# Joining the gating values and the second input projection into one program part, in a two-block kernel on one Trainium2 core

## The chip, the core and the metric

The kernel runs on one core of a Trainium2 chip. A core has five engines with their own instruction queues: TensorE (PE in the profile, its weight loads PEld), VectorE (DVE), ScalarE (ACT), GpSimd (POOL) and SyncE (SP, which here only issues DMAs). They meet at semaphores. The metric is the device time of one execution in microseconds (us); lower is better. Three runs of the kernel before took 3345.0, 3327.26 and 3340.97 us, with a median of 3340.97. The profiled execution took 3344.58 us, of which the trace spans 3342.8.

## The reference

Two residual blocks work on x, 2048 tokens of width 1024. The first is banded attention beside a multi-scale pooling, each gated; the second is a long convolution (Hyena) beside a spatial gating unit (SGU). Cut to what matters:

```python
def first_block(x, ...):
    h = rmsnorm(x, pre_norm_g)
    q, k, v, g_a, u_p, g_p = split(h @ w_in)
    a = banded_attention(q, k, v, rel_bias, attn_sink) * silu(g_a)
    p = multiscale_pool(u_p, pool_w, pool_scale) * silu(g_p)
    mixed = concat([a, p]) @ w_out                # "first output projection"
    return x + rmsnorm(mixed, post_norm_g)

def second_block(x, ...):
    proj = rms_norm(x, pre_norm_w) @ w_in         # 1024 -> 7168
    hy_in, hy_gate, sg_u, sg_v, sg_gate = split(proj)
    x0, x1, v = split(short_conv_centred(hy_in, conv_w, conv_b))
    k = hyena_filter(L, ...)      # three sine layers of width 64, exact to fp32
    y_a = x0 * long_conv_bidir(v * x1, k, hyena_skip) * silu(hy_gate)
    vn = normalise sg_v over the 128 values of each head
    y_b = sg_u * (sgu_w @ vn + sgu_b) * silu(sg_gate)
    return x + rms_norm(concat([y_a, y_b]) @ w_out, post_norm_w)
```

All is fp32. To multiply in TensorE's one-pass format (fp32r) without losing digits, an operand is split into a high part (ScalarE copies it to the format) and a low part (VectorE subtracts the copy from the value), and a product becomes three matmuls: high·high, low·high, high·low.

## The kernel before

The program is a row of parts. Each part is one block in which all engines run their own list of instructions; between two blocks stands a barrier. The parts are `first_block`, then two blocks in `second_inputs` (the gating values; the second input projection), `long_convolution` and `output`.

**End of `first_block`: the first output projection.** The 2048 tokens are 16 groups of 128 (`NT`). For group i TensorE runs `mix`, 48 matmuls of 128x512 (L849 to L851) into two of four banks of PSUM, then the 8 transposes (L729) of the *previous* group. After `mix` of a group ScalarE squares and sums (L520), GpSimd makes the reciprocal root from it (L400, L403), VectorE scales (L706) and adds the residual (L709, `x1_done`). Then ScalarE squares again (L522), GpSimd makes the second root, ScalarE scales (L526, `hs_done`), TensorE transposes, and VectorE takes the transposed tokens out of PSUM (L541). The features of group i+2 are split on the way: ScalarE copies (`features_high`, L492, L493; the second half comes from a scratch in DRAM by the DMA L362) and VectorE subtracts (`features_low`, L676, L677). VectorE also does 6 or 7 operations per group of `first_layer` (a sine for the filter net, L944 to L960), which have nothing to do with the tokens but must be done by the end of the part. The order of all of it is that of the code. Before the first `mix`, features and weights of the output projection are split (`weights_high` L485, `weights_low` L672), while the last of the 32 attention steps still runs: ScalarE takes the turned probabilities out of PSUM (L505), TensorE multiplies them (L832), VectorE gates the result (`gate`, L658).

**`second_inputs`, first block: gating values.** 32 steps (2 halves of 512 columns, 16 token groups) of 24 matmuls each (L1384 to L1386) go into one of six banks of PSUM in turn. VectorE takes mean and variance (L1353, L1358), GpSimd the root (L1282, L1284), VectorE the offset (L1367, `nb_done`), ScalarE normalises four heads out of PSUM (L1313, `vn_done`), SyncE stores. In the steps VectorE also does `SV_OPS[s]` operations of the filter's second layer (`filter_op`: L109 to L132, 631 in all); SyncE loads their rows (L66).

**`second_inputs`, second block: projection.** 49 tiles in a list: for each of 8 heads `gate`, `u`, `mix`, then for each of 8 groups `x0`, `hgate`, `x1`, `v`, with `third` (the filter's third layer) before the last group's. A tile of weights is 96 matmuls (L1665 to L1667) into four banks; tiles take banks 0 to 3 and 4 to 7 in turn. The weights (`WR`, two slots) are split two tiles ahead: ScalarE L1508, VectorE L1562. VectorE works on each tile (L1572, L1575, L1599 to L1615) and then does `OPS_BY[kind]` filter operations (13, for `mix` 6); whatever is left of the 631 it does at `x0` of group 6, and there `second_angle` follows (L1580, L1677 to L1687, L1582).

The SBUF place of the split value weights (`WVH`, `WVL`) is handed to the split weights of the projection (`WH2`, `WL2`) and to its buffers (`MB`) when the first of the two blocks ends.

Of the kernel before, what the change touches and what calls it, by code (L numbers as in the profile page):

```python
# [13 lines left out]
P = 128  # L14
# [120 lines left out]
def first_block(nc, A, M, WOH, WOL, FH, FL, PS, x1_d, h1_d, h2_d):  # L135


    with ExitStack() as ctx:
# [288 lines left out]
        def _(s):  # L427
# [69 lines left out]
            for st, (n, g) in enumerate(STEPS):  # L497
# [17 lines left out]
            for i in range(NT):  # L515
# [13 lines left out]
        def _(v):  # L529
# [169 lines left out]
            for i in range(NT):  # L699
# [397 lines left out]
def second_inputs(nc, A, PS, behind, CC, HP, kept, h1_d, h2_d, vn_d, bi_d, u_d, gx_d, yb_d):  # L1097

    with ExitStack() as outer:
# [84 lines left out]
        with ExitStack() as ctx:  # L1184
            def stage_sem(name):
                return ctx.enter_context(nc.semaphore(name))

# [3 lines left out]
            const_in = stage_sem("c2_in")  # L1191
            bias_in = stage_sem("bias2_in")
            hh_in = [stage_sem("hh_in%d" % i) for i in range(4)]
            high_done = stage_sem("high_done")
            low_done = stage_sem("low_done")
            sv_done = stage_sem("sv_done")
            quarter_done = stage_sem("quarter_done")
            stats_done = stage_sem("stats_done")
            var_done = stage_sem("var_done")
            rstd_done = stage_sem("rstd2_done")  # L1200
            nb_done = stage_sem("nb_done")
            vn_done = stage_sem("vn_done")
            vn_stored = [stage_sem("vn_stored%d" % i) for i in range(2)]
            bias_mm = stage_sem("bias2_mm")
            bias_done = stage_sem("bias2_done")
            bias_stored = stage_sem("bias2_stored")

            STEPS = 2 * NT
            block = ctx.enter_context(nc.Block())

            @block.sync
            def _(sp):
# [54 lines left out]
                for b in range(2):  # L1267
                    sp.wait_ge(vn_stored[b], 16 * NT)
                sp.wait_ge(bias_stored, 16)

            @block.gpsimd
            def _(g):
# [13 lines left out]
            @block.scalar  # L1286
            def _(s_):
# [27 lines left out]

            @block.vector
            def _(v):
# [21 lines left out]
                for s in range(STEPS):  # L1339
                    if s == 6:  # L1340
                        v.wait_ge(bias_mm, 2)
                        v.wait_ge(bias_in, 48)
                        for x in range(2):
                            v.tensor_tensor(BIA[:, 4 * x:4 * x + 4], PS[:, 6 + x, :].rearrange("p (a b) -> p a b", b=P),
# [3 lines left out]
                    if s in (NT - 1, NT):  # L1348
                        values_low(4 + 2 * (s - NT + 1))
                        values_low(5 + 2 * (s - NT + 1))  # L1350
                    v.wait_ge(sv_done, s + 1)
                    for a in range(4):
                        v.bn_stats(ST[:, a], PS[:, s % 6, P * a:P * a + P]).then_inc(stats_done, 1)  # L1353
# [16 lines left out]
            @block.tensor  # L1370
            def _(t):
                def quarter(s, q):
# [8 lines left out]
                    dst = PS[:, s % 6, :]  # L1381
# [1199 lines left out]
```

## Time and profile before

| | |
|---|---|
| Median of 3 runs | 3340.97 us (3327.26 to 3345.0) |
| Profiled execution | 3344.58 us, span 3342.8 us |
| TensorE busy | 3086.8 us, 92% of the span |
| VectorE busy | 2504.9 us, 75% |
| ScalarE busy | 804.9 us, 24% |
| GpSimd busy | 299.0 us, 9% |
| First output projection | from about 793.7 to 1027.6 us |
| Gating values | TensorE from 1045.7 to about 1239.1 us |
| Projection | TensorE from 1257.7 to about 2377 us |

Busy shares are means over parts with different limits. In a row of the trace, the number in square brackets is how long the engine stood idle before the instruction, and the name behind the arrow is the engine, tile and line that ended this wait. PEclk (granted clock) is 1.00 where TensorE runs at 2.4 GHz and 0.50 where it runs at 1.2 GHz; in between it is a mixture of the two.

### The profile page before, as it was taken

What the parts mean: (1) busy time and instruction counts of PE and PEld (TensorE: products, weight loads), DVE (VectorE), ACT (ScalarE), POOL (GpSimd) and SP (SyncE); (2) the same over time, 40 slices, a digit from 0 to 9 for tenths busy, and PEclk for the clock granted to TensorE, in tenths of its full rate; (3) what the DMA queues carried; (4) which work ended last, traced back from release to release, by engine and by line L of the source; (5) the groups of instructions that cost most, each with busy time, mean ns of one, the idle gap of its engine ahead of it and who ended that gap; (6) DMA issues with size and microseconds to landing.
All of it is one profiled execution on the core that took longest, in us unless ns stands there. A gap on an engine that the chain in (4) does not pass through costs nothing. (4 is left out here: it accounts for less than half of the span.)

```text
span 3342.8 us, 33360 instructions
## 1 busy us (share of the span) xinstructions
PE 3086.8 (92%) x13138; PEld 2238.6 (67%) x13138; DVE 2504.9 (75%) x2672; ACT 804.9 (24%) x1394; POOL 299.0 (9%) x420
## 2 busy tenths in 40 slices
PE   6999999889885989999999999999898999979999
PEld 4444444656774767787888888787566666777887
DVE  6979999597995796999999999975456667552221
ACT  2000000585333321000011111112353735431110
POOL 3211220000112350000000000000000000000000
PEclk9999999999997999999999999999999999979999
DMA  6565551201437454665545454521211120334321
GB/s 202 145 178 149 141 149 44 108 1 54 133 129 225 136 151 120 162 179 156 162 139 145 136 141 134 143 76 34 112 54 51 54 101 13 138 116 142 100 88 53
DMA packets 206060, 392.21 MB, mean 117 GB/s; under 512 B 20224, under 2 KB 132032, under 8 KB 198032
## 3 DMA queue, kind: packets, MB, share of 16 engines
q1 hardware_dynamic: 186000, 319.27, 31.2%
q0 software_dynamic: 18752, 62.42, 7.3%
q10 hardware_dynamic: 1152, 8.39, 0.7%
q8 instruction: 104, 1.70, 0.2%
q14 instruction: 52, 0.43, 0.0%
HBM read 312.41 MB, written 81.81 MB: 118 GB/s over the span
## 5 line engine op out<-in xcount | busy, mean ns | idle before, releaser
L1665 PE MATMUL PS<-HH,WH 128*128 128x512 f32 x1536 | 605.4, 394 | 40.2 <-DVE WL L1562 23.0
L1667 PE MATMUL PS<-HH,WL 128*128 128x512 f32 x1536 | 604.9, 394 | 0.0
L1666 PE MATMUL PS<-HL,WH 128*128 128x512 f32 x1536 | 604.2, 393 | 0.0
L782 PE MATMUL PS<-M 128*128 128x512 f32 x1152 | 502.3, 598 | 16.2 <-DVE M L605 13.6
L782 PEld LDWEIGHTS PS<-M 128*128 128x128 f32 x1152 | 220.4, 192 | 297.4 <-issue 279.8
L1665 PEld LDWEIGHTS PS<-HH,WH 128*128 128x128 f32 x1536 | 290.2, 189 | 110.3 <-DVE WL L1562 19.0
L1666 PEld LDWEIGHTS PS<-HL,WH 128*128 128x128 f32 x1536 | 290.2, 189 | 64.1
L1667 PEld LDWEIGHTS PS<-HH,WL 128*128 128x128 f32 x1536 | 290.3, 189 | 62.9
L109 DVE SCALAR_TENSOR_TENSOR HP<-MF,HP 128x1024 f32<-128x1024 f32 x252 | 323.4, 1283 | 8.0
L2394 PE MATMUL PS<-WH,YH 128*128 128x512 f32 x512 | 200.9, 392 | 14.7 <-DVE WL L2365 9.5
L109 DVE SCALAR_TENSOR_TENSOR M<-M 128x1024 f32<-128x1024 f32 x160 | 205.6, 1285 | 7.2 <-DMA M<-c_feat 1.5
L2395 PE MATMUL PS<-WH,YL 128*128 128x512 f32 x512 | 200.5, 392 | 0.0
L2396 PE MATMUL PS<-WL,YH 128*128 128x512 f32 x512 | 200.3, 391 | 0.0
L2354 DVE TENSOR_TENSOR YL<-KX,YH 128x2048 fp32r<-128x2048 f32 x14 | 32.1, 2292 | 209.3 <-ACT YH L2323 209.3
L1547 ACT ACTIVATE MB<-PS,MF 128x2048 f32<-128x2048 f32 x24 | 49.5, 2064 | 473.8 <-PE PS L1667 435.4
L2045 DVE TENSOR_TENSOR M<-PS,M 128x1024 f32<-128x1024 f32 x64 | 78.4, 1225 | 108.8 <-ACT M L1935 107.9
L2163 PE MATMUL PS<-M 128*128 128x256 f32 x512 | 131.4, 398 | 7.1 <-issue 4.2
L66 POOL DMA_DIRECT2D M<-c_feat x194 | 99.2, 516 | 383.5 <-DVE M L109 361.9
L1384 PE MATMUL PS<-WVH,HH 128*128 128x512 f32 x256 | 103.2, 403 | 28.2 <-DVE HL L1332 23.3
L2394 PEld LDWEIGHTS PS<-WH,YH 128*128 128x128 f32 x512 | 97.0, 189 | 35.3 <-DVE WL L2365 9.7
L2163 PEld LDWEIGHTS PS<-M 128*128 128x128 f32 x512 | 92.2, 188 | 41.7 <-issue 25.1
L2311 POOL MEMSET NEGH<- 128x1 f32 x1 | 0.1, 98 | 1337.3 <-POOLq L1692 1337.3
(220 smaller groups left out, 5110.7 us busy)
## 6 DMA issues: line engine op xcount, KB each, us to landing
MF<-h_scratch SPq DMA_DIRECT2D x380, 256.0 KB, 4.3
M<-c_feat POOLq DMA_DIRECT2D x194, 256.0 KB, 4.3
MF<-w_in SPq DMA_DIRECT2D x56, 512.0 KB, 4.7
M<-u_scratch SPq DMA_DIRECT2D x16, 1024.0 KB, 4.8
M<-w_in SPq DMA_DIRECT2D x18, 512.0 KB, 4.8
M<-x SPq DMA_DIRECT2D x16, 512.0 KB, 4.4
x_scratch<-M SPq DMA_DIRECT2D x16, 512.0 KB, 5.3
h_scratch<-M SPq DMA_DIRECT2D x16, 512.0 KB, 5.8
```

The source lines that it names most:

```text
L66: eng.dma_start(dst[HID * half:HID * half + HID], row).then_inc(loaded, 16)
L109: return v.scalar_tensor_tensor(out=out, in0=a, scalar=s_, in1=b, op0=op0, op1=op1)
L782: ins = t.matmul(PS[:, banks + c, :], wt[:, k], HT[:, k, TC * c:TC * c + TC], start=(k == 0), stop=(k == KD - 1))
L1384: t.matmul(dst, hh, wh, start=(k == 0), stop=False)
L1665: t.matmul(dst, wh, hh, start=(k == 0), stop=False)
L1666: t.matmul(dst, wh, hl, start=False, stop=False)
L1667: ins = t.matmul(dst, wl, hh, start=False, stop=(k == KD - 1))
L2045: v.tensor_tensor(PM, PS[:, bank:bank + 2, :], KS[:, n % 2], ALU.mult).then_inc(pm_done, 1)
L2163: return t.matmul(PS[:, bank, at:at + CH], STRIP[:, 2 * p + x, HID * strip:HID * strip + P], src[:, p, x], start=True, stop=True)
L2394: t.matmul(dst, yh, wh, start=(k == W_ORDER[0]), stop=False)
L2395: t.matmul(dst, yl, wh, start=False, stop=False)
L2396: return t.matmul(dst, yh, wl, start=False, stop=(k == W_ORDER[-1]))
```

## The change

It has three parts.

1. In the first output projection, ScalarE splits the features of group i+2 right behind L520 instead of behind L522, and VectorE does 3 of its 6 or 7 sine operations ahead of `features_low` and the rest behind it. Before the first `mix`, only group 0 and weight part 0 are split ahead of the last attention step; part 1 and group 1 come behind it on both engines.
2. Gating values and projection become one block. The values use banks 2 to 7 instead of 0 to 5 (`2 + s % 6`), the bias banks 0 and 1. In the last value step ScalarE and VectorE split the projection's first two weight tiles as soon as TensorE has finished the quarter of `WVH`/`WVL` whose place they take. TensorE's first tile waits for banks 2 and 3 by `vn_done`. GpSimd and SyncE wait for the last stores of the values before they load into the same places.
3. `SV_OPS` falls from 72 to 52 filter operations in the value steps.

```diff
@@ first_block, scalar
                 if st == len(STEPS) - 2:
...
-                    for i in range(2):
-                        features_high(i)
-                        weights_high(i)
+                    features_high(0)
+                    weights_high(0)
+            weights_high(1)
+            features_high(1)
...
                 s.activation(HS[:, i % 2], ps, ACT.Square, accum_out=SSQ[:, i:i + 1]).then_inc(mssq_done, 1)
+                if i + 2 < NT:
+                    features_high(i + 2)
                 s.wait_ge(x1_done, i + 1)
                 s.activation(HS[:, i % 2], X1[:, i % 2], ACT.Square, accum_out=SSQ2[:, i:i + 1]).then_inc(x1ssq_done, 1)
-                if i + 2 < NT:
-                    features_high(i + 2)
@@ first_block, vector
             gate(len(STEPS) - 2)
-            for i in range(2):
-                features_low(i)
-                weights_low(i)
+            features_low(0)
+            weights_low(0)
             gate(len(STEPS) - 1)
+            weights_low(1)
+            features_low(1)
...
                     features_out(i - 1)
+                first_layer_work(3)
                 if i + 2 < NT:
                     features_low(i + 2)
-                first_layer_work(7 if i < 7 else 6)
+                first_layer_work(4 if i < 7 else 3)
@@ second_inputs, values; scalar and vector
+                    if s == STEPS - 1:
+                        ahead_of_last()
...
-                        s_.activation(CN[s % 2][:, P * a:P * a + P], PS[:, s % 6, P * a:P * a + P], ACT.Identity,
+                        s_.activation(CN[s % 2][:, P * a:P * a + P], PS[:, 2 + s % 6, P * a:P * a + P], ACT.Identity,
@@ values, tensor
-                    if s == NT - 1:
+                    if s in (NT - 1, STEPS - 1):
                         ins.then_inc(quarter_done, 1)
@@ projection, sync
+                values_sync(sp)
...
                 raw_next(0)
                 raw_next(1)
+                for b in range(2):
+                    sp.wait_ge(vn_stored[b], 16 * NT)
@@ projection, gpsimd
+                values_gpsimd(g)
+                for b in range(2):
+                    g.wait_ge(vn_stored[b], 16 * NT)
+                g.wait_ge(sv_done, STEPS)
@@ projection, scalar
-                weights_high(0)
-                weights_high(1)
+                def first_high():
+                    for w in range(2):
+                        s.wait_ge(quarter_done, 5 + w)
+                        weights_high(w)
+
+                values_scalar(s, first_high)
@@ projection, vector
-                weights_low(0)
-                weights_low(1)
+                def first_low():
+                    for w in range(2):
+                        v.wait_ge(quarter_done, 7 + w)
+                        weights_low(w)
+
+                values_vector(v, first_low)
@@ projection, tensor
+                            if j == 0:
+                                t.wait_ge(bias_done, 2)
+                                if c >= 2:
+                                    t.wait_ge(vn_done, 4 * (STEPS - 3 + c))
...
-SV_OPS = [0] * 8 + [3] * 24
+SV_OPS = [0] * 8 + [3] * 8 + [2] * 12 + [1] * 4
```

Three places in the engines' orders follow. The line numbers of the kernel after are up to 16 higher: L520 is L521 there, L522 is L525, L526 is L527, L706 is L708, L709 is L711, L953 is L956, L1313 is L1307, L1508 is L1510, L1562 is L1568, L1353 is L1348. Rows name an instruction and its output and inputs; M is the first block's SBUF buffer, FH and FL are the high and low parts of features, WH and WL those of projection weights, MF and HP hold filter data.

VectorE, first output projection, one token group, before:

```order
L706 SCALAR_TENSOR_TENSOR M<-PS,M 128x1024
L709 TENSOR_TENSOR M<-M 128x1024
L541 TENSOR_TENSOR M<-PS,M 128x1024
L676 TENSOR_TENSOR FL<-M,FH 128x512
L677 TENSOR_TENSOR FL<-FL,FH 128x512
L953 TENSOR_TENSOR M<-M 128x1024 x3
L957 TENSOR_SCALAR M<-M 128x1024
```

And after:

```order
L708 SCALAR_TENSOR_TENSOR M<-PS,M 128x1024
L711 TENSOR_TENSOR M<-M 128x1024
L542 TENSOR_TENSOR M<-PS,M 128x1024
L956 TENSOR_TENSOR M<-M 128x1024 x3
L677 TENSOR_TENSOR FL<-M,FH 128x512
L678 TENSOR_TENSOR FL<-FL,FH 128x512
L960 TENSOR_SCALAR M<-M 128x1024
```

Three sine operations now stand between L541 and the two subtractions of the features.

VectorE, the last two value steps and the start of the projection, before:

```order
L1353 BN_STATS MF<-PS 128x6 x4
L1358 BN_AGGR MF<-MF 128x2 x4
L130 TENSOR_TENSOR MF<-MF,HP 128x1024
L132 TENSOR_TENSOR MF<-HP,MF 128x1024
L109 SCALAR_TENSOR_TENSOR HP<-MF 128x1024
L1367 SCALAR_TENSOR_TENSOR MF<-MF 128x4
L1184 UNCONDITIONAL_BRANCH
L1553 UNCONDITIONAL_BRANCH
L1562 TENSOR_TENSOR WL<-MF,WH 128x1024 x3
```

And after:

```order
L132 TENSOR_TENSOR MF<-HP,MF 128x1024
L1362 SCALAR_TENSOR_TENSOR MF<-MF 128x4
L1568 TENSOR_TENSOR WL<-MF,WH 128x1024 x2
L1348 BN_STATS MF<-PS 128x6 x4
L1353 BN_AGGR MF<-MF 128x2 x4
L109 SCALAR_TENSOR_TENSOR HP<-MF 128x1024
L1362 SCALAR_TENSOR_TENSOR MF<-MF 128x4
L1568 TENSOR_TENSOR WL<-MF,WH 128x1024
```

The branches into the next block are gone, the first two weight tiles stand ahead of the last step's statistics, and one filter operation is left in the step instead of three.

VectorE, projection, tile `x0` of group 6, before:

```order
L1572 SCALAR_TENSOR_TENSOR MB<-PS,MF,MB 128x2047
L1575 SCALAR_TENSOR_TENSOR MB<-PS,MF,MB 128x2047
L1562 TENSOR_TENSOR WL<-MF,WH 128x1024
L1580 TENSOR_SCALAR MF<-MF 128x1024
L1677 TENSOR_SCALAR HP<-MF 128x1024
```

And after:

```order
L1578 SCALAR_TENSOR_TENSOR MB<-PS,MF,MB 128x2047
L1581 SCALAR_TENSOR_TENSOR MB<-PS,MF,MB 128x2047
L1568 TENSOR_TENSOR WL<-MF,WH 128x1024
L132 TENSOR_TENSOR MF<-HP,MF 128x1024
L109 SCALAR_TENSOR_TENSOR HP<-MF 128x1024
L116 TENSOR_TENSOR HP<-HP,MF 128x1024
L118 TENSOR_TENSOR MF<-HP 128x1024
L120 TENSOR_TENSOR MF<-MF 128x1024
L109 SCALAR_TENSOR_TENSOR HP<-MF,HP 128x1024 x4
L130 TENSOR_TENSOR MF<-MF,HP 128x1024
L132 TENSOR_TENSOR MF<-HP,MF 128x1024
L1586 TENSOR_SCALAR MF<-MF 128x1024
```

Eleven filter operations now stand between the weights and `second_angle`; nine more stand at the tile ahead of it (`v` of group 5: 13 instead of 4).

## Rows read from the trace of the kernel before

**Rows 1.** Windows: start:end, length, busy of PE PEld DVE ACT POOL, PEclk, DMA share, GB/s

```profile
1239.10:1257.70 18.60, 0.03 (x1) 0.00 (x0) 11.91 (x28) 6.83 (x15) 8.16 (x7) 0.62 0.51 142
2123.45:2213.86 90.41, 88.40 (x385) 71.96 (x385) 88.38 (x65) 11.86 (x9) 0.00 (x0) 1.00 0.44 122
```

**Rows 2.** Timeline, VectorE, one token group of the first output projection

```profile
880.36 1.28 DVE L706 SCALAR_TENSOR_TENSOR M<-PS,M 128x1024 f32<-128x1024 f32 x1
...
885.16 0.69 DVE L676 TENSOR_TENSOR FL<-M,FH 128x512 fp32r<-128x512 f32 x1 [1.12 <-ACT FH L493]
...
886.37 8.77 DVE L953 TENSOR_TENSOR M<-M 128x1024 f32<-128x1024 f32 x7
895.18 1.28 DVE L706 SCALAR_TENSOR_TENSOR M<-PS,M 128x1024 f32<-128x1024 f32 x1
```

**Rows 3.** Groups of instructions, VectorE, 810 to 1010 us: busy, mean ns, idle before

```profile
L676 DVE TENSOR_TENSOR FL<-M,FH 128x512 fp32r<-128x512 f32 x14 | 9.7, 693 | 16.8 <-ACT FH L493 16.8
```

**Rows 4.** Timeline, ScalarE's scaling in group 5 and in group 14

```profile
885.03 1.15 ACT L526 ACTIVATE M<-M 128x1024 f32<-128x1024 f32 x1
1010.41 1.15 ACT L526 ACTIVATE M<-M 128x1024 f32<-128x1024 f32 x1 [2.79 <-POOL M L403]
```

**Rows 5.** Timeline, GpSimd's root in group 5 and in group 14

```profile
884.45 0.55 POOL L403 TENSOR_TENSOR M<-M 128x1 f32<-128x1 f32 x1
1008.84 1.53 POOL L403 TENSOR_TENSOR M<-M 128x1 f32<-128x1 f32 x1
```

**Rows 6.** Timeline, VectorE, starts of groups 14 and 15

```profile
1003.89 1.28 DVE L706 SCALAR_TENSOR_TENSOR M<-PS,M 128x1024 f32<-128x1024 f32 x1
1015.50 1.28 DVE L706 SCALAR_TENSOR_TENSOR M<-PS,M 128x1024 f32<-128x1024 f32 x1 [0.50 <-POOL M L403]
```

**Rows 7.** DMA issues: KB each, median us to landing, of the features' second half

```profile
FL<-pt_scratch SPq DMA_DIRECT2D x16, 256.0 KB, 5.9
```

**Rows 8.** Timeline, ScalarE and TensorE, last attention step

```profile
787.81 0.62 ACT L492 ACTIVATE FH<-M 128x512 fp32r<-128x512 f32 x1
789.79 0.64 ACT L505 ACTIVATE M<-PS 128x256 f32<-128x256 f32 x2
790.22 1.12 PE L811 MATMUL PS<-M 128*128 128x128 f32 x4 [2.63 <-ACT M L505]
```

**Rows 9.** Timeline, VectorE, first value step: statistics to offset

```profile
1069.52 0.89 DVE L1353 BATCH_NORM_STATS2 MF<-PS 128x6 f32<-128x128 f32 x4 [11.02 <-PE PS L1386]
1073.13 0.17 DVE L1367 SCALAR_TENSOR_TENSOR MF<-MF 128x4 f32<-128x4 f32 x1 [1.19 <-POOL MF L1284]
```

**Rows 10.** Timeline, ScalarE and TensorE, from the values to the projection

```profile
1250.11 1.50 ACT L1313 ACTIVATE CN<-PS,MF 128x128 f32<-128x128 f32 x4 [3.60 <-DVE MF L1367]
1255.36 2.00 ACT L1508 ACTIVATE WH<-MF 128x1024 fp32r<-128x1024 f32 x2 [3.75 <-PEq L1184]
1257.73 0.80 PE L1665 MATMUL PS<-HH,WH 128*128 128x512 f32 x1 [18.60 <-DVE WL L1562]
1281.39 1.88 ACT L1526 ACTIVATE MB<-PS 128x2048 f32<-128x2048 f32 x1 [22.73 <-PE PS L1667]
```

**Rows 11.** Timeline, VectorE, projection, groups 5 and 6

```profile
2122.08 1.22 DVE L1562 TENSOR_TENSOR WL<-MF,WH 128x1024 fp32r<-128x1024 f32 x1
2140.08 2.35 DVE L1572 SCALAR_TENSOR_TENSOR MB<-PS,MF,MB 128x2047 f32<-128x2047 f32 x1
2212.49 1.22 DVE L1562 TENSOR_TENSOR WL<-MF,WH 128x1024 fp32r<-128x1024 f32 x1
2218.78 2.35 DVE L1572 SCALAR_TENSOR_TENSOR MB<-PS,MF,MB 128x2047 f32<-128x2047 f32 x1
2238.04 2.29 DVE L1615 TENSOR_TENSOR MB<-MB 128x2048 f32<-128x2048 f32 x1 [2.60 <-ACT MB L1534]
```

**Rows 12.** Timeline, ScalarE, behind tiles hgate and x1 of group 6

```profile
2236.12 1.88 ACT L1534 ACTIVATE MB<-PS 128x2048 f32<-128x2048 f32 x1 [20.45 <-PE PS L1667]
2258.10 2.06 ACT L1547 ACTIVATE MB<-PS,MF 128x2048 f32<-128x2048 f32 x1 [19.15 <-PE PS L1667]
```

More of the change, by code:

```diff
@@ L1190, in second_inputs, with values_sync @@
             CN = [CC[:, 0:TC], sbuf(ctx, "CN", [TC], F32)[:, :]]
[L1191 to L1206, printed above, removed]
+            const_in = sem("c2_in")
+            bias_in = sem("bias2_in")
+            hh_in = [sem("hh_in%d" % i) for i in range(4)]
+            high_done = sem("high_done")
+            low_done = sem("low_done")
+            sv_done = sem("sv_done")
+            quarter_done = sem("quarter_done")
+            stats_done = sem("stats_done")
+            var_done = sem("var_done")
+            rstd_done = sem("rstd2_done")
+            nb_done = sem("nb_done")
+            vn_done = sem("vn_done")
+            vn_stored = [sem("vn_stored%d" % i) for i in range(2)]
+            bias_mm = sem("bias2_mm")
+            bias_done = sem("bias2_done")
+            bias_stored = sem("bias2_stored")
             STEPS = 2 * NT
-            block = ctx.enter_context(nc.Block())
-            @block.sync
-            def _(sp):
+            def values_sync(sp):
                 def values_load(c):
@@ L1266, in _, with values_gpsimd @@
                         weight_load(sp, 1)
[L1267 to L1272, printed above, removed]
+            def values_gpsimd(g):
                 g.sem_clear(behind)
@@ L1284, in _, with values_scalar @@
                     g.tensor_tensor(RSTD[:, s % 2], RSTD[:, s % 2], NEGH, ALU.pow).then_inc(rstd_done, 1)
-            @block.scalar
-            def _(s_):
+            def values_scalar(s_, ahead_of_last):
                 def values_high(c):
@@ L1312, in _, with values_vector @@
                     for a in range(4):
-                        s_.activation(CN[s % 2][:, P * a:P * a + P], PS[:, s % 6, P * a:P * a + P], ACT.Identity,
+                        s_.activation(CN[s % 2][:, P * a:P * a + P], PS[:, 2 + s % 6, P * a:P * a + P], ACT.Identity,
                                       bias=NB[:, s % 2, a:a + 1], scale=RSTD[:, s % 2, a:a + 1]).then_inc(vn_done, 1)
-            @block.vector
-            def _(v):
+            def values_vector(v, ahead_of_last):
                 def values_low(c):
@@ L1343, in _ @@
                         for x in range(2):
-                            v.tensor_tensor(BIA[:, 4 * x:4 * x + 4], PS[:, 6 + x, :].rearrange("p (a b) -> p a b", b=P),
+                            v.tensor_tensor(BIA[:, 4 * x:4 * x + 4], PS[:, x, :].rearrange("p (a b) -> p a b", b=P),
                                             SGBA[:, 4 * x:4 * x + 4], ALU.add).then_inc(bias_done, 1)
@@ L1350, in _ @@
                         values_low(5 + 2 * (s - NT + 1))
+                    if s == STEPS - 1:
+                        ahead_of_last()
                     v.wait_ge(sv_done, s + 1)
                     for a in range(4):
-                        v.bn_stats(ST[:, a], PS[:, s % 6, P * a:P * a + P]).then_inc(stats_done, 1)
+                        v.bn_stats(ST[:, a], PS[:, 2 + s % 6, P * a:P * a + P]).then_inc(stats_done, 1)
                     v.wait_ge(stats_done, 4 * s + 4)
@@ L1368, in _, with values_tensor @@
                                            op0=ALU.mult, op1=ALU.mult).then_inc(nb_done, 1)
-            @block.tensor
-            def _(t):
+            def values_tensor(t):
                 def quarter(s, q):
@@ L1380, in quarter @@
                         t.wait_ge(wl_done, 4 * half + q + 1)
-                    dst = PS[:, s % 6, :]
+                    dst = PS[:, 2 + s % 6, :]
                     for k in (2 * q, 2 * q + 1):
@@ L1393, in values @@
                         ins = quarter(s, q)
-                    if s == NT - 1:
-                        t.wait_ge(quarter_done, 4)
+                    if s in (NT - 1, STEPS - 1):
+                        t.wait_ge(quarter_done, 4 * (s // NT + 1))
                         t.sem_inc(sv_done, 1)
@@ L1412, in _ @@
                     for a in range(4):
-                        ins = t.matmul(PS[:, 6 + x, P * a:P * a + P], SNBA[:, 4 * x + a], SGTA[:, 4 * x + a], start=True, stop=True)
+                        ins = t.matmul(PS[:, x, P * a:P * a + P], SNBA[:, 4 * x + a], SGTA[:, 4 * x + a], start=True, stop=True)
                     ins.then_inc(bias_mm, 1)
@@ L1628, in _ @@
             def _(t):
+                values_tensor(t)
                 def banks_free(j):
```

2 lines of the change are left out of this document (removed).

## The prediction

> **What bounds the kernel now.** I read the windows by stage first, then VectorE's timeline in the first output projection, then the three engines around the barrier between values and projection, and last VectorE's timeline near the end of the filter work, because that is where moved work must come out again. TensorE is busy 92% of the span, so what is left to win are its waits; each part has its own.
>
> In the first output projection VectorE sets the pace. One token group (group 5) runs from 880.36 to 895.18, 14.82 us, and in it VectorE stands idle once, 1.12 us, for ScalarE's copy of the features; the seven sine operations after it are back to back, and the next group starts at once [rows 2]. Over the stretch these waits are 16.8 us in 14 pieces, the first of them longer than the others [rows 3].
>
> Between values and projection TensorE stands 18.60 us. ScalarE normalises the last step at 1250.11 and begins the first weight tile of the next block at 1255.36; TensorE starts at 1257.73 [rows 10]. The window over the gap shows a granted clock of 0.62, so TensorE fell from 2.4 to 1.2 GHz in it [rows 1], and the first tile took 1281.39 - 1257.73 = 23.66 us [rows 10] where a regular one takes 2258.10 - 2236.12 = 21.98 [rows 12].
>
> In the projection both engines are full: in the 90.41 us of one group of four tiles TensorE is busy 88.40 and VectorE 88.38 [rows 1]. There is no room for more VectorE work until the filter is done. That comes at `x0` of group 6; from L1615 on VectorE waits, the first time 2.60 us [rows 11].
>
> **The change part by part.** Sums are made against the profiled execution, 3344.58 us.
>
> *Start of the output projection.* ScalarE took the last step's probabilities out at 789.79; the second batch of splitting ahead of it began at 787.81 [rows 8]. With the batch behind it, they come out 1.98 us sooner, and TensorE, which waited 2.63 us for them [rows 8], goes on sooner by as much. What could be late next is the weights: weight part 1 and one features split now stand behind VectorE's gate. A part serves 6 matmuls, 21.98 / 16 = 1.37 us at full clock, and VectorE makes one in about 1.2 us, so it keeps ahead except at the first parts, where TensorE's clock has just come out of a wait. Bounds 0 and 2.0, a little more if the clock no longer falls in the wait; I take -2.0, since the chain is plain.
>
> *ScalarE's copies ahead of L522, three sine operations ahead of `features_low`.* This takes the 16.8 us [rows 3] off VectorE: the copies are done while it works on the group before. All its instructions stay. What is late next:
> - GpSimd's second root. In group 5 it took 0.55 us in its second instruction, and ScalarE scaled at 885.03, 4.67 us after the group's start; in group 14, which has no features to wait for, VectorE was working meanwhile, the same instruction took 1.53, and ScalarE scaled 1010.41 - 1003.89 = 6.52 us after the start [rows 2, 4 to 6]. VectorE will now always be working there, so I take 6.52. The next group can start at the earliest 1015.50 - 1010.41 = 5.09 us later (the next square, its root), 11.61 after its forerunner, as group 15 did, with 0.50 of idle time [rows 6]. VectorE itself needs 14.82 - 1.12 = 13.70 us with seven sine operations and 1.25 less, 12.45, with six [rows 2]. It stays the slowest by 0.8.
> - TensorE. `features_low` ends at 3.68 (885.16 - 1.12 - 880.36) + 3 x 1.25 + 1.21 = 8.6 us after the group's start, the transposes about when 6.52 + 1.15 + 1 = 8.7. Its own work is 48 matmuls (half a tile, 11.0) and the transposes (about 1): 12.0, under 12.45.
> I take 16.8 less 0.3, for group 1's and group 15's roots, which now show: -16.5. Bounds: -16.8, and 0 if the chain of roots takes over (below).
>
> The Trainium skill has a rule that speaks against this step: by the GPSIMD Engine Reference, Key points, GpSimd shares its SBUF interfaces with VectorE and contends with VectorE instructions that have two SBUF inputs. The trace agrees (0.55 against 1.53 us). Were the rule without effect the chain would be 9.8 instead of 11.6, and the sum the same, since 12.45 is above both.
>
> *Joining the blocks.* TensorE ends the values at 1257.73 - 18.60 = 1239.13 [rows 10]; the last step of 24 matmuls (5.5 us) begins at 1233.6. With one filter operation per step VectorE no longer lags, so step 30 goes as in the first step: 1073.13 - 1069.52 = 3.61 us from the statistics to the offset, with one operation of that size between [rows 9], then 0.2 and 1.50 for ScalarE's normalising [rows 10]: 1238.9. Only then does ScalarE come to the new first weight tile (its queue is in order; the tile's place has been free since 1235). From ScalarE's start to TensorE's it was 1257.73 - 1255.36 = 2.37 us [rows 10]: 1241.3. TensorE stands 2.2 us instead of 18.6: -16.4. I take it that the clock then holds, and the tile 1.7 us shorter: -18.1 together. What else waits there: banks 2 and 3 need steps 30 and 31 normalised, 1238.9 and about 1248, while TensorE wants them 11 and 16.5 us after 1241.3. SyncE's loads for tiles 2 and 3 stand behind the last store (about 1248) and are wanted after tile 0, at 1263; GpSimd's loads for `mix` stand behind the stores' landing and are wanted at 1285. Bounds: -14 (the root as slow as with a busy VectorE, and the clock falls) and -20.3 (no gap at all).
>
> *Twenty filter operations moved.* In the values they cost nothing: TensorE sets the pace there. In the projection the full price is 20 x 1.30 = 26 us of VectorE. (1.30: from weights to next taps it is 18.00 us with 13 operations, 6.29 with 4 [rows 11], so 11.7 for nine.) Up to `v` of group 5 every tile has the same number as before. There it is 13 instead of 4: the taps of `x0` 6 go from 2218.78 to 2230.5. The weights of `x1` are then ready at 2230.5 + 2 x 2.35 + 1.2 = 2236.4 or so, TensorE wants them at 2236.1: 0.5 late. From these taps to L1615 it was 2238.04 - 2.60 - 2218.78 = 16.66; with 11 more operations (14.3) L1615 is at 2261.5 and the weights of `v` are ready at 2261.5 + 2.2 + 1.2 = 2264.9. TensorE ends `x1` at 2258.6, so it stands 6.3 us; before it went on at 2258.1 [rows 12]. That is +6.8, and +1.7 for the clock after such a wait: +8.5. From there VectorE has slack of over 10 us per tile. Bounds: +5 (half of it, if the clock holds and operations pair better) and +27.7 (all 26 and the clock).
>
> Sum: -2.0 - 16.5 - 18.1 + 8.5 = **-28.1 us**, 3316.5 for an execution like the profiled one. The median of the runs shown is 3.6 us below that one, so I predict 3340.97 - 28.1 = **3312.9 us**.
>
> **Rivals.**
> 1. *The moved operations come at full price.* For it: VectorE is at 88.38 of 90.41 us. Against: the idle time after L1615 takes up what isn't due earlier. -2.0 - 16.5 - 18.1 + 27.7 = -8.9: 3332 us.
> 2. *The roots' chain takes VectorE's place in the first output projection.* For it: margin of only 0.8 us, and GpSimd's time changes with what VectorE does [rows 5]. Against: group 14 shows the chain with VectorE busy, 11.61. At 13.6 us a group nothing is won: -11.6, 3329 us.
> 3. *The seam opens less than it seems*, because another wait (the table load, a load behind the stores, step 31's normalising) holds the first tiles. About 12 us of the 18 lost: -16, 3325 us.
> 4. *Slower: ScalarE waits for the features' DMA.* The copies now stand ahead of L522, and their second half needs a DMA that is issued when `mix` of the group before ends, 8.7 + 11.0 - 12.45 = 7.3 us into the group. With a landing of 5.9 us [rows 7] and 0.6 for the copy ScalarE is free at 13.8, 1.3 into the next group, and L522 is wanted at 2.5. So a landing of 7.1 us is where it begins to cost, every microsecond above it 14 times. At 11 us it is 14 x 3.9 = 55: +27, 3368 us. Against: 5.9 was measured with three other transfers in flight; the DMA now goes out alone.
>
> **How the numbers follow.** The forecast 0.72 (its own range 3304 to 3321), rivals 1, 2 and 3 0.08 each, rival 4 0.03, 0.01 for the rest. The range of 8 in 10 takes in part of the rivals and the runs' own scatter: 3301 to 3328. A difference under 0.5% (16.7 us) can't be told from none. Faster by more than that (below 3324.3) are the forecast, nearly all of it, and a good third of rivals 2 and 3 in milder form: 0.79. Within: 0.18. Slower: 0.03.
>
> **What would show it.** VectorE: no idle time ahead of the features' subtraction, groups of 13.7 and 12.4 us, ScalarE's scaling 6.5 us into the group. Seam: TensorE idle 2 to 3 us, first tile near 22 us. Group 6: TensorE's wait for the weights of `v` about 6 us, TensorE at 1.2 GHz for the first matmuls behind it. Wrong would be: VectorE waiting for GpSimd at L706 in most groups, ScalarE waiting for the DMA ahead of L493's copy, waits of TensorE for L1562 in the gate, u and mix tiles longer than before, or a seam over 6 us.

## The result and the profile after

The kernel after takes **3314.22 us** (median of 8 runs, 3298.07 to 3317.83), the one before 3335.47 (8 runs, 3326.84 to 3345.0). The ratio is 0.9926, 95% interval 0.9903 to 0.995. The profiled execution took 3317.83 us (span 3316.0) against 3344.58 (span 3342.8): -26.75, where the sum had said -28.1. Of the sixteen runs of before beside experiments 1 to 4 and 7, one took 12136.62 us; it is left out, and the median given there is that of the other fifteen.

| place | before | after | moved by | forecast |
|---|---|---|---|---|
| near the end of attention (gate of the fifth step from the last) | 778.76 | 780.40 | +1.64 | none |
| first group of the output projection begins | 808.36 | 807.24 | -2.76 | -2.0 |
| its sixteenth group begins | 1015.50 | 996.23 | -18.15 | -16.5 |
| TensorE begins the values | 1045.67 | 1026.18 | -0.22 | none |
| TensorE ends the values | 1239.13 | 1222.02 | +2.38 | none |
| TensorE begins the projection | 1257.73 | 1224.15 | -16.47 | -16.4 |
| end of its tile 0 | 1281.39 | 1246.43 | -1.38 | -1.7 |
| end of `v`, group 6 | 2280.08 | 2254.05 | +8.93 | +8.5 |
| long convolution begins | 2387.32 | 2361.01 | -0.28 | none |
| end of the span | 3342.8 | 3316.0 | -0.5 | none |

The fourth column is what the stretch up to that place gave or took by itself; its sum is -26.8.

**A group of the output projection.** VectorE's timeline of one after (start in us, duration in us, engine and line, operation, out<-in, partitions x elements, count, and in brackets the idle time before it with what ended it):

```profile
872.03 1.28 DVE L708 SCALAR_TENSOR_TENSOR M<-PS,M 128x1024 f32<-128x1024 f32 x1
873.35 1.23 DVE L711 TENSOR_TENSOR M<-M 128x1024 f32<-128x1024 f32 x1
874.49 1.22 DVE L542 TENSOR_TENSOR M<-PS,M 128x1024 f32<-128x1024 f32 x1
875.63 3.74 DVE L956 TENSOR_TENSOR M<-M 128x1024 f32<-128x1024 f32 x3
879.40 0.69 DVE L677 TENSOR_TENSOR FL<-M,FH 128x512 fp32r<-128x512 f32 x1
880.01 0.68 DVE L678 TENSOR_TENSOR FL<-FL,FH 128x512 fp32r<-128x512 f32 x1
880.61 4.99 DVE L956 TENSOR_TENSOR M<-M 128x1024 f32<-128x1024 f32 x4
885.64 1.28 DVE L708 SCALAR_TENSOR_TENSOR M<-PS,M 128x1024 f32<-128x1024 f32 x1
```

L677 has no bracket: the 1.12 us of before [rows 2] are gone, and the group takes 885.64 - 872.03 = 13.61 us instead of 14.82. ScalarE's scaling and GpSimd's root in it, and VectorE where the last group begins:

```profile
878.55 1.15 ACT L527 ACTIVATE M<-M 128x1024 f32<-128x1024 f32 x1 [2.78 <-POOL M L403]
```

```profile
876.98 1.53 POOL L403 TENSOR_TENSOR M<-M 128x1 f32<-128x1 f32 x1
```

```profile
996.23 1.28 DVE L708 SCALAR_TENSOR_TENSOR M<-PS,M 128x1024 f32<-128x1024 f32 x1 [0.50 <-POOL M L403]
```

The scaling comes 878.55 - 872.03 = 6.52 us into the group, where it came after 4.67 [rows 2, 4], and the root takes 1.53 us, where it took 0.55 [rows 5]. In this group before, the root ran while VectorE stood idle for the copy; now VectorE is in the middle of its sine operations. The later scaling costs nothing, since VectorE needs 12.35 us and more. Only the sixteenth group waits, by the same 0.50 as before [rows 6].

ScalarE now waits ahead of its copies, which it did not do before:

```profile
882.30 0.63 ACT L492 ACTIVATE FH<-M 128x512 fp32r<-128x512 f32 x1 [1.60 <-issue]
```

"issue" means that the profile shows no releaser. The wait is for the DMA of the features' second half: issued at 878.39, it landed at 882.23, 0.07 us ahead of this row, and in 13 of the 14 groups the copy starts 0.07 to 0.08 us behind the landing. The waits are 26.0 us in sum, none above 2.5. They cost nothing, because both copies end at 883.5, before ScalarE's second square of the next group can start, at 888.2.

**The seam.** ScalarE, VectorE and TensorE, in that order, around the end of the values:

```profile
1220.32 1.51 ACT L1307 ACTIVATE CC<-PS,MF 128x128 f32<-128x128 f32 x4 [2.84 <-DVE MF L1362]
1221.70 2.01 ACT L1510 ACTIVATE WH<-MF 128x1024 fp32r<-128x1024 f32 x2
...
1246.43 1.88 ACT L1532 ACTIVATE MB<-PS 128x2048 f32<-128x2048 f32 x1 [14.57 <-PE PS L1683]
```

```profile
1222.87 2.36 DVE L1568 TENSOR_TENSOR WL<-MF,WH 128x1024 fp32r<-128x1024 f32 x2 [2.59 <-ACT WH L1510]
```

```profile
1224.15 0.50 PE L1681 MATMUL PS<-HH,WH 128*128 128x512 f32 x1 [2.13 <-DVE WL L1568]
```

The chain is the same as in [rows 10], from ScalarE's copy to TensorE 1224.15 - 1221.70 = 2.45 us, but it begins before TensorE is done with the values, not 16 us behind. The first matmul takes 0.50 us, where it took 0.80 [rows 10], and the window (columns as in [rows 1]) shows the full grant, 2.4 GHz, where [rows 1] had 0.62. That the clock held is this execution's; experiments 5 and 7 have the same wait and lost it (below).

```profile
1218.00:1224.00 6.00, 4.03 (x18) 2.89 (x16) 2.17 (x3) 3.40 (x6) 1.94 (x2) 1.00 0.28 96
```

**Group 6 of the projection**, where the moved filter work comes out: VectorE, then TensorE, then the clock.

```profile
2195.41 2.35 DVE L1578 SCALAR_TENSOR_TENSOR MB<-PS,MF,MB 128x2047 f32<-128x2047 f32 x1
2197.79 2.35 DVE L1581 SCALAR_TENSOR_TENSOR MB<-PS,MF,MB 128x2047 f32<-128x2047 f32 x1
2200.18 1.23 DVE L1568 TENSOR_TENSOR WL<-MF,WH 128x1024 fp32r<-128x1024 f32 x1
2201.32 1.22 DVE L132 TENSOR_TENSOR MF<-HP,MF 128x1024 f32<-128x1024 f32 x1
...
2226.15 2.28 DVE L1625 TENSOR_TENSOR MB<-MB 128x2048 f32<-128x2048 f32 x1
2228.35 1.22 DVE L1568 TENSOR_TENSOR WL<-MF,WH 128x1024 fp32r<-128x1024 f32 x1
```

```profile
2201.55 0.47 PE L1681 MATMUL PS<-HH,WH 128*128 128x512 f32 x1 [0.48 <-DVE WL L1568]
2229.72 0.77 PE L1681 MATMUL PS<-HH,WH 128*128 128x512 f32 x1 [5.94 <-DVE WL L1568]
```

```profile
2231.00:2244.00 13.00, 13.00 (x51) 10.46 (x51) 5.54 (x3) 1.48 (x2) 0.00 (x0) 0.88 0.36 103
```

Between the weights of `x1` (2200.18) and those of `v` (2228.35) VectorE has 24.8 us of filter work without a gap. TensorE waits 0.48 us for the first and 5.94 for the second, and begins behind the second at 0.77 us a matmul, 1.2 GHz. In a group before that nothing has changed: the same 90.4 us as in [rows 1] give 88.40 and 88.37.

```profile
2103.00:2193.40 90.40, 88.40 (x386) 71.96 (x385) 88.37 (x65) 11.86 (x8) 0.00 (x0) 1.00 0.49 134
```

### The profile page after: what moved, and what is told of

Read it like the earlier page. It is cut to its first block and busy times, and to the rows that moved or that the text cites. A ratio compares the mean times of both kernels' runs of the same rounds, so it can differ in the third digit from the quotient of the medians.

```text
span 3316.0 us, 33371 instructions
## 1 busy us (share of the span) xinstructions
PE 3086.2 (93%) x13138; PEld 2234.5 (67%) x13138; DVE 2503.2 (75%) x2672; ACT 808.8 (24%) x1394; POOL 325.4 (10%) x420
## 5 line engine op out<-in xcount | busy, mean ns | idle before, releaser
L1378 PE MATMUL PS<-WVH,HH 128*128 128x512 f32 x256 | 104.3, 407 | 27.2 <-DVE HL L1325 22.3
```

Of the source, the lines that this page charges most:

```text
L1378: t.matmul(dst, hh, wh, start=(k == 0), stop=False)
```

## The experiments

Every set of runs has its own runs of the kernel before beside it. They lie in two clusters, some 15 us apart, as do those of after and of several kernels below; experiments 8 to 11 are about these. A single execution is compared by stages, not by its total.

**1 and 2. The first block alone.** Starts and groups of the output projection as after; the two old program parts and the old row of filter operations.

```
 weights_high(1)
 features_high(1)
...
-SV_OPS = [0] * 8 + [3] * 8 + [2] * 12 + [1] * 4
+SV_OPS = [0] * 8 + [3] * 24
```

> Only the first part of the change: the new order of splitting and sine operations in the first output projection; two blocks, old SV_OPS. My theory: its gain stands by itself, since the next part begins behind a barrier. From the trace after, the groups run 18.2 us faster and the start about 2.8, so the projection of values begins 20 to 21 us sooner in relation to the attention, the gap of 18.6 us between the blocks stays, and the total is 17 to 21 us under before. Rival (the roots' chain takes over, or the gain is given back at the barrier by late transfers): under 12 us.

Measured: 3314.29 us (median of 10), before 3331.74, ratio 0.9948 (0.9929 to 0.9967). The sixteen groups begin within 189.01 us, as after (188.99), and the seam stays: TensorE waits 18.36 us at 1222.57. But from there to the wait of group 6 it took 1037.85 us, before 1029.23, though no wait is longer than in before and the full clock is shown; the tiles of group 6 took 22.40 us. So the same kernel ran again.

> The same kernel as the first experiment (the first block's new order alone), looked at again for the second projection's tiles, which took 22.4 instead of 22.0 us there with no wait and a full clock shown. Theory (a property of that execution or chip, not of the kernel): the tiles take 22.0 us, first L1668 to the end of the projection 1029 to 1031 us, and the execution is 3305 to 3309 us, or 3321 to 3325 with the late store. Rival (it belongs to this kernel's code): again 22.4 us and 1037 to 1038.

Measured: 3308.6 us, and

```profile
1221.61 0.80 PE L1668 MATMUL PS<-HH,WH 128*128 128x512 f32 x1 [18.55 <-DVE WL L1565]
...
2250.84 0.79 PE L1668 MATMUL PS<-HH,WH 128*128 128x512 f32 x1 [5.02 <-DVE MB L1578]
```

2250.84 - 1221.61 = 1029.23, as before. So the lost 8.6 us belonged to that execution, not to the code: 28 of its tiles in a row ran at 0.233 us a matmul (start to start) instead of 0.229. The second execution has three such tiles, the other traces none to three; what makes a tile 22.40 us in one stretch and 21.98 in another stays open. The first block's part is worth what its stages say, some 21 us (2.76 + 18.15): 3308.6 is 21 us below 3329.75, the middle of the lower cluster of before beside it. The seam and the moved operations give the rest.

**3. The join with the old row of filter operations.**

```
-SV_OPS = [0] * 8 + [3] * 8 + [2] * 12 + [1] * 4
+SV_OPS = [0] * 8 + [3] * 24
```

> The changed kernel with SV_OPS as before (72 filter operations in the value steps, none moved). My theory: VectorE is then some 10 us behind TensorE at the end of the values, and since the split of the first weight tile stands behind its steps, TensorE waits 9 to 10 us at the seam instead of 2.1, with the clock fallen (first tile 23.7 instead of 22.3 us); in return the wait of 5.9 us at v of group 6 is gone. Sum within 3 us of the changed kernel. Rival (moved operations cost their full 26 us): 15 us or more faster than the changed kernel.

Measured: 3298.57 us (median of 7), before 3331.74, ratio 0.9919 (0.9886 to 0.9951).

```profile
1213.20 0.80 PE L1681 MATMUL PS<-HH,WH 128*128 128x512 f32 x1 [9.70 <-DVE WL L1568]
```

With the old row TensorE still waits 9.70 of the 18.6 us: three operations a step keep VectorE late with the statistics, so ScalarE begins to normalise step 30 only at 1209.37, 5.9 us behind the end of the values (1203.51), and its copies are in order behind that. In group 6 the wait for `v` is gone. So the new row trades 7.6 us and a fallen clock at the seam for 5.9 us and a fallen clock in group 6. The two kernels differ by less than these runs can tell.

**4 and 5. Which half of the group's new order does it.** One kernel has ScalarE's two copies behind the second square again, the other VectorE's two rests ahead of all sine operations.

```
 s.activation(HS, ps, Square)
-features_high(i + 2)
 ...
 s.activation(HS, X1, Square)
+features_high(i + 2)
```

```
-first_layer_work(3)
 features_low(i + 2)
-first_layer_work(4 if i < 7 else 3)
+first_layer_work(7 if i < 7 else 6)
```

> The changed kernel with ScalarE's copies of the features behind the second square again, as before; VectorE keeps three sine operations ahead of the subtraction. My theory: VectorE asks for the copies about 7.4 us into a group and they are done at 4.8, so the 16.8 us of waits stay gone, and GpSimd's second root runs beside a busy VectorE all the same: time and group periods as in the changed kernel (13.6 and 12.35 us). Rival (the copies' early place is what counts): waits of about 1 us a group come back.

> The new block of the output projection's groups with ScalarE's two copies ahead of the two squares, but VectorE's three rests (L677) ahead of all seven of its sine operations, as before the change. Theory (the wait was for ScalarE's copies, and either half alone removes it): no row of L677 waits, the groups keep the periods of after (12.5 and 13.6 us), first to sixteenth L708 within 1 us of 189.0, and the span lies within 4 us of that with VectorE's half alone (3296.4) or, with the late store, 16 to 19 us above. Rival (the halves are not equal: with the rests early VectorE still waits for the second copy, some 1 to 3 us in a group, because both copies need the first square's end): L677 waits 8 to 20 us in sum and the span is longer by that.

Measured: 3298.23 and 3301.9 us, one run each. Groups of instructions on VectorE over the output projection (busy, mean ns, idle before), first of the one with VectorE's half, then of the one with ScalarE's:

```profile
L677 DVE TENSOR_TENSOR FL<-M,FH 128x512 fp32r<-128x512 f32 x14 | 9.7, 692 | 0.5
```

```profile
L677 DVE TENSOR_TENSOR FL<-M,FH 128x512 fp32r<-128x512 f32 x14 | 9.5, 682 | 0.0
```

In [rows 3] it was 16.8 us of idle time. First to sixteenth group take 189.02 and 188.97 us: either half alone brings the whole gain, and the other adds nothing to it. One edit closes the gap between copy and use, whichever side moves; the rival that the halves are unequal fell.

**6. The seam's last 2 us.** ScalarE makes the first weight tiles' copies one value step earlier.

```
-if s == STEPS - 1:
+if s == STEPS - 2:
     ahead_of_last()
```

> After, with one condition changed: ScalarE makes the high halves of the first two weight tiles of the joined section at the last step but one of the values instead of the last. Theory (the 2.1 us at the seam are the tail of a chain ScalarE scaling, ScalarE copies, VectorE rests, and nothing else): TensorE's wait ahead of the first L1681 is 0 to 0.5 us, the clock stays 1.00, and first L1681 to the end of tile 0 is 22.0 to 22.3 us; worth 1.6 to 2.1 us. Rival (the weights' DMA or VectorE's rests are the later condition): the wait stays over 1.5 us. Everything else as in after.

Measured, one run of 3296.42 us:

```profile
1201.65 0.47 PE L1681 MATMUL PS<-HH,WH 128*128 128x512 f32 x1 [0.30 <-PE PS L1380]
```

The wait goes from 2.13 to 0.30, and what ends it is TensorE's own last matmul of the values. Nothing but ScalarE's place in its queue held it. The three other kernels with this edit (experiments 9 to 11) show the same 0.30.

**7. The wait in group 6.** The filter's second pair of sines, 10.7 us of VectorE (2215.48 to 2226.15), is made one tile later, in the gate of group 6.

```
 if (kind, n) == ("x0", 6):
     filter_work(v, OPS_OF(HID))
-    second_angle()
+elif (kind, n) == ("hgate", 6):
+    second_angle()
```

> The changed kernel with second_angle moved from x0 of group 6 to hgate of group 6, behind its gating and its weights. My theory: the 5.9 us that TensorE waits for the weights of v of group 6 is the angle's 10.7 us standing ahead of them, not the moved filter operations as such; with the angle behind, the weights are ready before TensorE ends x1, the wait is 0 to 0.5 us and the clock doesn't fall: 7 to 9 us faster than the changed kernel. Rival (VectorE's total work up to the third tile sets the time): the wait comes back at the next tile and under 3 us are won.

Measured: 3294.89 us (median of 4), before 3331.74, ratio 0.9884 (0.9846 to 0.9922). ScalarE behind `v` of group 6, here and in the kernel of experiment 4, which began the projection within 0.2 us of it:

```profile
2231.21 2.06 ACT L1553 ACTIVATE MB<-PS,MF 128x2048 f32<-128x2048 f32 x1 [15.13 <-PE PS L1684]
```

```profile
2238.62 2.06 ACT L1553 ACTIVATE MB<-PS,MF 128x2048 f32<-128x2048 f32 x1 [21.62 <-PE PS L1683]
```

The wait of 5.9 us and its slow matmuls are gone, -7.4, and the long convolution begins 7.1 us sooner. Of the moved operations' cost this is nearly all: from the first matmul of the projection to the long convolution it is 1130.13 us here and 1129.59 in before, both with a fallen clock in the first tile. The moved operations cost because, with the second pair of sines, they stand ahead of the weights of `v`, not because VectorE lacks the time.

This kernel and that of experiment 4 also show that the wait at the seam can go either way with the clock. After the same 2.13 us the first matmul took 0.50 us there and 0.80 here:

```profile
1208.02 0.80 PE L1682 MATMUL PS<-HH,WH 128*128 128x512 f32 x1 [2.12 <-DVE WL L1568]
```

Tile 0 took 22.3 us there, in after and in experiment 8, and 23.8 here and in experiment 5.

**8 and 9. Two clusters.** The last two sets have 22 runs of before: 10 at 3326.08 to 3332.39, 12 at 3341.65 to 3349.09. After has 6 at 3314 to 3318 and 2 at 3298. Both profiled executions belong to the upper one. VectorE in the first projection, before and after:

```profile
189.86 4.69 DVE L583 TENSOR_TENSOR M<-M 128x2079 f32<-128x2079 f32 x2 [17.41 <-DMA pt_scratch<-M]
```

```profile
192.39 4.68 DVE L584 TENSOR_TENSOR M<-M 128x2079 f32<-128x2079 f32 x2 [19.41 <-DMA pt_scratch<-M]
```

It waits for the 1-MB store of pooled features, which landed 18.2 and 20.3 us after its issue at 171.58 and 171.97. In those of experiments 1 to 7 it landed in 5.0 to 5.1 us (issue at 170.60 to 171.02) and VectorE waited 2.7 or less. At the same moment SyncE issues a 4-MB copy of the output weights inside DRAM (18 us). The idea was that the copy alone makes the store late.

```
-if j == 6:
+if j == 7:
     sp.dma_start(wo_d, A["w_out"][0])
```

> After with one edit: the 4-MB copy of the output weights (L341) is issued one projection tile later. Theory (the two clusters of times, 3298 and 3314 us, come from the 1-MB store of pooled features landing in 5 or in 18 to 20 us, the latter when the copy starts at the same moment): all executions lie in 3294 to 3300, L584 never waits for the store, and the store lands in 4.5 to 6 us. Rival (something else makes the store late): both clusters remain. Rival B (the copy disturbs another load at its new place): one cluster, but above 3300.

> After with three edits: the second sine pair of group 6 made in the tile of its gate (as in the run with the second angle at hgate), the first weight tiles split one step early, and the 4-MB copy of the output weights issued one projection tile later, away from the store of the pooled features. Theory: each takes away its own wait, 7.2, about 2 and, in the executions that have the late store, 15 to 17 us; so all executions lie in one cluster, at 3288 to 3295 us, and the ratio to before is 0.986 to 0.989. Rival A (the late store has another cause than the copy beside it): times stay two-valued, 3290 and 3306. Rival B (the copy at its new place delays the loads of the projection's weights or the second store by as much): one cluster at 3300 to 3310.

Measured: 3307.7 us (4 runs, 3302.07 to 3314.28), and with the edits of experiments 6 and 7 added 3295.25 (6 runs, 3291.09 to 3304.53), before 3341.65, ratios 0.9905 (0.9874 to 0.9937) and 0.9868 (0.984 to 0.9897). Neither theory held. The first is as its rival B said, everything above 3300; the second is two-valued, four runs at 3291 to 3296 and two at 3304, near what its rival A said. VectorE of the first, then of the second:

```profile
217.63 1.28 DVE L109 SCALAR_TENSOR_TENSOR M<-M 128x1024 f32<-128x1024 f32 x1 [1.37 <-DMA M<-c_feat]
219.98 2.60 DVE L109 SCALAR_TENSOR_TENSOR M<-M 128x1024 f32<-128x1024 f32 x2 [1.07 <-DMA M<-c_feat]
```

```profile
181.30 4.68 DVE L584 TENSOR_TENSOR M<-M 128x2079 f32<-128x2079 f32 x2 [8.52 <-DMA pt_scratch<-M]
...
216.73 3.92 DVE L109 SCALAR_TENSOR_TENSOR M<-M 128x1024 f32<-128x1024 f32 x3 [7.16 <-DMA M<-c_feat]
```

At its new place the copy holds up GpSimd's loads of the filter's features instead: those issued within 3 us behind it took 14 to 18 us, undisturbed ones some 4. And the second execution still had the late case, smaller: 9.4 us for a store with no copy beside it. What all four late ones share (before, after, experiment 9, experiment 10) is their start. The first 192 matmuls of the first projection (that of the first block), of after and of experiment 6:

```profile
56.13 84.36 PE L785 MATMUL PS<-M 128*128 128x512 f32 x192 [1.32 <-DVE M L542]
```

```profile
56.71 82.67 PE L785 MATMUL PS<-M 128*128 128x512 f32 x192 [1.32 <-DVE M L542]
```

84.36 us in each of the four, 82.67 in each of the other nine; the window 56 to 83.4 shows a granted clock of 0.94 and of 1.00. The store waits for TensorE, GpSimd's loads for VectorE. With the slow start the store is issued behind the first of the loads (load 170.70, store 171.97 in after), otherwise ahead of them (store 171.02, load 171.16 in experiment 6). That this order makes it late is argued from the times, not tried; why the clock falls at the start in some executions stays open.

**10 and 11. Copy after the last tile, and the same kernel with the copy where it was.** Both have the edits of experiments 6 and 7.

```
-if j == 6:
+if j == n1 - 1:
     sp.dma_start(wo_d, A["w_out"][0])
```

> After with the second sine pair of group 6 made in the tile of its gate, the first weight tiles split a step early, and the 4-MB copy of the output weights issued at the last tile of the first projection (some 490 us, where the DMA share falls to 0.4 and then 0). What the runs so far showed of the late case: TensorE starts the first projection with a fallen clock (first 192 matmuls in 84.4 instead of 82.7 us), so the store of pooled features is issued behind GpSimd's loads, and VectorE, which has no slack there, waits 8.5 us for it without the copy beside it and 19.4 us with it; a copy moved by one tile makes VectorE wait at the second store. Theory: with the copy far away the early case is as in the run with the split a step early or a little better, 3287 to 3293 us, and the late one 8 to 11 us above it (3296 to 3303) instead of 16. Rival: the late store doesn't depend on the copy; the clusters stay 15 to 17 us apart.

> As the run with the copy after the last tile, but with the copy where the kernel after has it. Theory: two clusters, 3288 to 3294 and 3304 to 3310 us. Rival: the seam's edit gives back 2 us and no more, the second angle's is hidden: 3292 to 3298 for the early cluster.

Measured: with the copy late 3293.75 us (6 runs, 3290.26 to 3296.68), with the copy in its old place 3291.41 (4 runs: 3284.54, 3291.03, 3291.79, 3307.73), before 3344.62; ratios 0.9862 (0.9835 to 0.9889) and 0.9862 (0.9827 to 0.9897). The profiled execution of the first has the slow start, and took 3293.61 all the same, where 3296 to 3303 was expected. The second kernel is two-valued as expected, but for the 3284.54 below its lower range. Rows of the first:

```profile
180.90 4.68 DVE L584 TENSOR_TENSOR M<-M 128x2079 f32<-128x2079 f32 x2 [8.14 <-DMA pt_scratch<-M]
...
437.34 2.93 PE L785 MATMUL PS<-M 128*128 128x512 f32 x3 [5.44 <-DVE M L606]
```

The second row is TensorE's. Without the copy the late store costs VectorE 8.14 us instead of 19.41, and TensorE, which VectorE feeds in this stretch, stands once, for 5.44. After had 8.71 and 5.45. The six runs lie within 6.4 us, and none is in an upper cluster; with the copy in its old place one of four is, at 3307.73. So the copy was most of the late store's price, not its cause; this rests on one trace with a slow start and on six runs. Both kernels are faster than after: their runs outside an upper cluster lie at 3284.5 to 3296.7, those of after at 3298.1 and 3298.7. The ratios (0.9862 against 0.9926) say more than that: the median of before beside them, 3344.62, lies in its upper cluster, the one beside after, 3335.47, between the two, and after had six of eight runs in its own upper one.

## Why the prediction was right

Predicted 3312.9, measured 3314.22; range and sign held. That the two lie within 1.3 us of each other is in part luck, since both medians, the 3340.97 it started from and that of after, came from the upper cluster. From the median of all eight runs of before, 3335.47, the same sum gives 3307.4. By its own steps:

- *Start of the output projection, -2.0.* Measured -2.76, from the gate of the fifth step from the last to the first group. The mechanism was right: TensorE's wait of 2.63 us [rows 8] became one of 0.80 and one of 0.35. TensorE began the projection 2.8 us sooner and at the full clock (1.00 in its first 6.5 us, 0.78 before), and gave some of that back in a wait of 0.68 us for weight part 2. The other kernels with this change show 26.7 to 26.9 us for the stretch, before shows 29.6.
- *The groups, -16.5.* Measured -18.15. The mechanism was right, VectorE stayed the slowest, and the size was 1.65 too small. Each of 13 groups got 1.20 to 1.22 shorter, the first 2.34, where the idle rows say 1.12 and 2.2. The other 0.09 is overlap: in a row without waits the next instruction begins before the record of the one ahead of it ends (875.63 against 874.49 + 1.22 = 875.71), and behind a wait it does not. So a wait cost its idle time and the lost overlap, 14 times. The 0.3 taken off for the roots was wrong: group 15 already waited 0.50 before. The Trainium skill's rule in the GPSIMD Engine Reference, Key points, that GpSimd contends with VectorE instructions with two SBUF inputs, fits the traces: the median of L403 rose from 0.56 to 1.53 us over the kernel. It cost nothing here.
- *The seam, -16.4 and -1.7.* Measured -16.47 and -1.38. Step 30 is normalised by 1220.32 + 1.51 = 1221.83, 0.2 us before TensorE ends the values, and the forecast had 1238.9 against 1239.13. The wait was right by its mechanism. The 1.7 was chance in part: it took it that the clock holds, and of five traces with this wait three kept it and two lost it, with a first tile of 22.3 or 23.8 us. And even at full clock tile 0 takes 22.3, not 21.98, as it is counted from a first matmul behind a wait.
- *Twenty operations moved, +8.5.* Measured +8.93, of it 5.94 + 0.48 wait (6.3 and 0.5 forecast). Experiments 3 and 7 show that it was this step and this place.
- *What it left out.* TensorE took 2.38 us longer for the values: the first 24 us of them had a granted clock of 0.79 against 0.93 before, then it is the same. The kernels of experiments 3 and 4 have the same code up to step 16 and show 0.93 and 0.86, those of 6 and 11, alike up to there too, 0.94 and 0.85. The kernel of experiments 1 and 2, one and the same, shows 0.85 and 0.92. So it is chance between executions, and the 1.64 us ahead of the first row of the table, where the change doesn't reach, are too. Windows with TensorE alone (length, busy, PEclk, DMA share, GB/s), before and after:

```profile
1045.67:1069.67 24.00, 20.79 (x80) 0.93 0.92 300
```

```profile
1026.18:1050.18 24.00, 21.57 (x73) 0.79 0.89 289
```

Rival 1 (full price, +27.7) fell by experiment 3: the row costs no more than it saves. Rival 2: the chain of roots shows nowhere but in group 15, and there as before. Rival 3: no other wait stood at the seam; experiment 6 takes the last 2 us. Rival 4: its condition came true and its price did not. ScalarE does wait for the features' DMA in every group, 1.6 to 2.5 us, which the prediction had named as a sign of being wrong. But the DMA was issued 6.4 us into the group, not 7.3, and landed in 3.8 us in the group shown, and in 3.0 by the median, where it had been 5.9 [rows 7]:

```profile
FL<-pt_scratch SPq DMA_DIRECT2D x14, 256.0 KB, 3.0
```

So ScalarE is free at 11.4 us in place of the 13.8 reckoned, and the next group needs it 2.5 us into its own time, at 16.1. The 14 waits cost nothing; no run shows from what landing on they would.

The largest thing the prediction had not seen was the noise. The profiled execution and two of before's three runs lay in the upper of two clusters. Of the eight runs of before beside after's, four are in each: upper to upper the medians differ by 28.5 us, lower to lower by 29.7. The forecast stands for that; the difference of the overall medians, 21 us, mixes the two, since after had six of eight in its upper one.

## What to carry to other kernels

Where an engine waits briefly for a copy in every group, moving either the copy ahead or its use behind can be enough, as it was here; price the chain that comes next with the neighbours busy, and find a group in the old trace where they already are. Work moved to where time is free comes out at the last due time behind it, so put what isn't due (here the second angle) behind that. When times lie in two clusters, compare the first rows that differ between two profiles before reading anything into a median.

## What the runs showed of the hardware that I had not expected

- A 1-MB store to DRAM landed in 5.0 to 5.2 us beside a 4-MB copy inside DRAM when issued just ahead of the loads, in 9.1 to 9.4 us behind two of them without the copy, and in 18.2 to 20.3 behind two of them with it.
- A wait of 2.13 us left the first matmul behind it at 0.50 us in after and in experiments 4 and 8 but at 0.80 (1.2 GHz) in experiments 7 and 5. The waits of 5.02 and 5.94 us in the projection were followed by one of 0.76 to 0.80 us in every trace that has them.
- Tiles of the same 96 matmuls took 21.98 or 22.40 us at a full granted clock, in one execution the longer time for 28 tiles in a row and 8.6 us more in sum; no cause found.
